# Reading a matmul's streamed columns in turns from two halves, and shifting seven weight buffers by 64 bytes

## The reference, cut to what matters

```
D_FF = 5632                                      # 44 tiles of 128
gate, up = split(h @ w_up, 2, axis=-1)           # h [256, 2048], w_up [2048, 11264]
return (gelu(dwconv_centred(gate)) * up) @ w_down    # w_down [5632, 2048]
```

## Time and profile before

| what | us |
|---|---|
| time of the kernel, median of two runs | 2174.7 (2173.54 and 2175.87) |
| span of the profiled execution | 2171.5 |
| TensorE busy with matmuls in it | 2132.8 (98%) |
| VectorE, ScalarE busy | 1464.8 (67%), 1037.6 (48%) |
| up-projection L, units 6 to 43 | about 1500 to 1920 of the span |
| down-projection M0 and M1 without the last unit | about 1920 to 2151 of the span |

### The profile page before, as it was taken

One profiled execution on the slowest core, in us unless ns is written; L12 is line 12 of the kernel. 1 busy time (PEld: TensorE's weight loads), 2 busy tenths in 40 slices (PEclk: granted clock), 3 DMA queues, 4 the chain that ended last, 5 costly groups with the idle time before them and its releaser, 6 DMA issues.

```text
span 2171.5 us, 38030 instructions
## 1 busy us (share of the span) xinstructions
PE 2132.8 (98%) x16496; PEld 1987.9 (92%) x16496; DVE 1464.8 (67%) x1850; ACT 1037.6 (48%) x1418; POOL 25.0 (1%) x47
## 2 busy tenths in 40 slices
PE   7999999999999999999999999999999999999998
PEld 7989999988999999998788999999999999988886
DVE  7666556666757698696665577789666665555665
ACT  6554334444454465454433455465444444444454
POOL 0000000110000000000000000000000000000000
PEclk9999999999999999999999999999999999999999
DMA  9765655775448878786565655766777775555553
GB/s 326 239 208 195 196 194 176 232 243 162 153 156 263 295 256 267 252 285 223 182 224 166 233 175 192 255 210 229 240 245 240 243 242 195 194 193 190 182 196 112
DMA packets 339156, 470.05 MB, mean 216 GB/s; under 512 B 14797, under 2 KB 312557, under 8 KB 326126
## 3 DMA queue, kind: packets, MB, share of 16 engines
q1 hardware_dynamic: 337838, 466.93, 64.5%
q0 software_dynamic: 1152, 0.70, 0.1%
HBM read 464.80 MB, written 2.10 MB: 215 GB/s over the span
## 4 chain that ended last, share of the span: by engine, by line
PE 91%; DVE 5%; ACT 2%; DMA 2%; issue 1%; SPq 0%; ACTq 0%; DVEq 0%
PE ps L1971 64%; PE ps L1982 11%; PE ps L1990 4%; DVE wlo L1191 2%; PE ps L2002 1%; PE ps L2060 1%; ACT whi L595 1%; DMA raw<-w_branch_dram 1%; PE ps L2321 1%; PE ps L2261 1%; PE ps L2223 1%; PE ps L2255 1%; DVE arena L1257 1%; DMA raw<-w_in_dram 1%; PE ps L1926 1%
## 5 line engine op out<-in xcount | busy, mean ns | idle before, releaser
L1191 DVE TENSOR_TENSOR wlo<-raw,whi 128x1024 fp32r<-128x1024 f32 (+1 forms) x668 | 814.6, 1221 | 661.7 <-ACT whi L595 658.5
L595 ACT ACTIVATE whi<-raw 128x1024 fp32r<-128x1024 f32 (+1 forms) x668 | 706.3, 1058 | 1065.2 <-PE ps L1971 860.5
L1971 PE MATMUL ps<-f_hi,whi 128*128 128x256 f32 x2112 | 422.0, 281 | 1.6 <-DVE f_lo L1835 1.6
L1971 PE MATMUL ps<-f_lo,whi 128*128 128x256 f32 x2112 | 413.8, 277 | 0.0
L1971 PE MATMUL ps<-f_hi,wlo 128*128 128x256 f32 x2112 | 413.5, 277 | 0.0
L1971 PEld LDWEIGHTS ps<-f_hi,whi 128*128 128x128 f32 x2112 | 320.7, 188 | 14.3 <-issue 11.8
L1971 PEld LDWEIGHTS ps<-f_hi,wlo 128*128 128x128 f32 x2112 | 319.9, 188 | 0.0
L1971 PEld LDWEIGHTS ps<-f_lo,whi 128*128 128x128 f32 x2112 | 319.9, 188 | 0.0
L1971 PE MATMUL ps<-phi,whi 128*128 128x256 f32 (+2 forms) x1440 | 300.7, 290 | 0.0
L1971 PE MATMUL ps<-plo,whi 128*128 128x256 f32 (+2 forms) x1440 | 288.4, 281 | 0.0
L1971 PE MATMUL ps<-phi,wlo 128*128 128x256 f32 (+2 forms) x1440 | 288.1, 281 | 0.0
(11 more groups left out here) (380 smaller groups left out, 2595.1 us busy)
## 6 DMA issues: line engine op xcount, KB each, us to landing
raw<-w_in_dram SPq DMA_DIRECT2D x151, 1024.0 KB, 5.9
raw<-ada_w_dram SPq DMA_DIRECT2D x96, 1024.0 KB, 5.0
raw<-ffn_w_up_dram SPq DMA_DIRECT2D x88, 1024.0 KB, 5.0
raw<-ffn_w_down_dram SPq DMA_DIRECT2D x44, 1024.0 KB, 5.2
raw<-w_out_dram SPq DMA_DIRECT2D x32, 1024.0 KB, 5.7
raw<-w_branch_dram SPq DMA_DIRECT2D x16, 1024.0 KB, 6.1
arena<-xT_dram SPq DMA_DIRECT2D x4, 544.0 KB, 6.6
arena<-ctxT_dram SPq DMA_DIRECT2D x1, 2048.0 KB, 11.1
```

Of the source, the lines that this page charges most:

```text
L595: nc.scalar.activation(whi[slot_of(c)][:, 0:w], src, ACT.Copy).then_inc(S("split_hi"), 1)
L1191: v.tensor_tensor(wlo[slot_of(c)][:, 0:w], src, whi[slot_of(c)][:, 0:w].bitcast(F32), ALU.subtract).then_inc(S("split_lo"), 1)
L1971: l = mm(ps[2 * p + h][0:m, b:b + tt.stop - tt.start], wx[:, k], x[:, xi, tt], start=first, stop=last)
```

## The change: order of the streamed columns, and buffers

1. In L, units 6 to 43, chunks q = 1 to 3, a matmul reads its 256 streamed columns no longer straight through. It reads a run from the first half of the tile, one from the second half, the next run of the first half, and so on. A run is 16 floats (64 bytes) for q = 1 and 2 and 4 floats (16 bytes) for q = 3. For q = 2 and 3 the sums are written to PSUM in the same order, so that each column lands where it did. For q = 1 the tiles `kt` 4 to 7 of `f_hi` and `f_lo` are stored in an order that makes the turned reading give the natural one, and PSUM is written straight.
2. In M0 and M1 (without the last unit) the same is done with the 512 streamed weight columns and the sums, for q = 1 to 3, with the same run lengths.
3. To store the four tiles so, ScalarE writes `f_hi` in a stepped pattern, and VectorE writes `f_lo` with two instructions of 128 columns in place of one of 256.
4. Slots 5 to 7 of `whi` and slots 4 to 7 of `wlo` start 64 bytes later, which is a multiple of 128 bytes. Slot 4 of `whi` stays. These buffers serve all phases from E on.

```diff
-        whi += [at(f"whi{4 + i}", [128, CW], MEM + RING * RW + CW * i + 16, F32R) for i in range(4)]
-        wlo += [at(f"wlo{4 + i}", [128, CW], MEM + RING * RW + CW * (4 + i) + 16, F32R) for i in range(4)]
+        whi += [at(f"whi{4 + i}", [128, CW], MEM + RING * RW + CW * i + (32 if i else 16), F32R) for i in range(4)]
+        wlo += [at(f"wlo{4 + i}", [128, CW], MEM + RING * RW + CW * (4 + i) + 32, F32R) for i in range(4)]
+
+        def turns(v, n):
+
+            return v.rearrange("p (two run n) -> p run two n", two=2, n=n)
@@ stream_hi
-                nc.scalar.activation(f_hi[:, kt, :], ptmp[:, kt % 2, 0:256], ACT.Identity, bias=shift).then_inc(S("res_hi"), 1)
+                src, dst = ptmp[:, kt % 2, 0:256], f_hi[:, kt, :]
+                if k == 1 and kt // 4 == 1:
+                    src, dst = src.rearrange("p (run two n) -> p run two n", two=2, n=16), turns(dst, 16)
+                nc.scalar.activation(dst, src, ACT.Identity, bias=shift).then_inc(S("res_hi"), 1)
@@ stream_lo
+                if k == 1 and kt // 4 == 1:
+                    src = ptmp[:, kt % 2, 0:256].rearrange("p (run two n) -> p two run n", two=2, n=16)
+                    hi, dst = f_hi[:, kt, :].rearrange("p (two run n) -> p two run n", two=2, n=16), f_lo[:, kt, :].rearrange("p (two run n) -> p two run n", two=2, n=16)
+                    v.scalar_tensor_tensor(dst[:, 0], src[:, 0], shift, hi[:, 0].bitcast(F32), ALU.add, ALU.subtract)
+                    v.scalar_tensor_tensor(dst[:, 1], src[:, 1], shift, hi[:, 1].bitcast(F32), ALU.add, ALU.subtract).then_inc(S("res_lo"), 1)
@@ chunk, the matmuls of T units
-                                l = mm(ps[2 * p + h][0:m, b:b + tt.stop - tt.start], wx[:, k], x[:, xi, tt], start=first, stop=last)
+                                moving, sums = x[:, xi, tt], ps[2 * p + h][0:m, b:b + tt.stop - tt.start]
+                                if name == "L" and not early and q:
+                                    moving = turns(moving, 4 if q == 3 else 16)
+                                    if q > 1:
+                                        sums = turns(sums, 4 if q == 3 else 16)
+                                l = mm(sums, wx[:, k], moving, start=first, stop=last)
@@ chunk, the matmuls of DN units (M0, M1)
-                                l = mm(ps[(4 if name == "M0" else 0) + 2 * t + nb][:, :], x[:, kd, 128 * t:128 * t + 128],
-                                       wx[:, 512 * nb:512 * nb + 512], start=first, stop=last)
+                                moving, sums = wx[:, 512 * nb:512 * nb + 512], ps[(4 if name == "M0" else 0) + 2 * t + nb][:, :]
+                                if q:
+                                    n = 4 if q == 3 else 16
+                                    moving, sums = turns(moving, n), turns(sums, n)
+                                l = mm(sums, x[:, kd, 128 * t:128 * t + 128], moving, start=first, stop=last)
```

More of the change, by code:

```diff
@@ L1698, in stream_lo @@
                 dve.wait_ge(S("res_hi"), 16 * k + kt + 1)
-                v.scalar_tensor_tensor(f_lo[:, kt, :], ptmp[:, kt % 2, 0:256], shift, f_hi[:, kt, :].bitcast(F32), ALU.add, ALU.subtract)\
-                    .then_inc(S("res_lo"), 1)
+                if k == 1 and kt // 4 == 1:
[3 more added lines that the diff above has]
+                    v.scalar_tensor_tensor(dst[:, 1], src[:, 1], shift, hi[:, 1].bitcast(F32), ALU.add, ALU.subtract).then_inc(S("res_lo"), 1)
+                else:
+                    v.scalar_tensor_tensor(f_lo[:, kt, :], ptmp[:, kt % 2, 0:256], shift, f_hi[:, kt, :].bitcast(F32), ALU.add, ALU.subtract)\
+                        .then_inc(S("res_lo"), 1)
                 dve.wait_ge(S("res_lo"), 16 * k + kt + 1)
```

## The result

The changed kernel takes 2224.4 us (median of two runs, 2221.39 and 2227.50) against 2174.7 us. The ratio is 1.0237, with a 95% interval of 1.0187 to 1.0287. So the change is clearly slower. The profiled execution has a span of 2225.7 us, 54.2 us more than the one before.

The account below looks back on a forecast made before the run. The prediction took TensorE's matmul pace as the bound and summed 0 + 10.1 + 1.1 + 3.5 + 1.0 = +15.7 us, taking 2174.7 to 2190 us. Its range was 2150 to 2250 us.

Parts of the forecast that it names:

- rival B: Turned reads in L, M0, M1: each change of place in memory costs time, 2220 to 2280 us; chance 0.26.
- last sign: Closing test: prediction wrong altogether if reads at a new order change the level by more than 4.5 ns.
- What bounds: Whole MLP stage: TensorE's matmul pace sets the time in both directions, in flight for 98% of the span.
- Term 1: Order of the turned reads in L, M0, M1: taken as 0, bounds -30.0 to +89.7 us.
- Term 2: Shifted buffers under turned reads in L: +3.7 ns a matmul, +10.1 us, and +1.1 us for q = 0.
- Term 3: Shifted buffers in E to OB, straight reads: low-pace chunks +5.3 us, the others -1.8 us, together +3.5 us.
- Term 4: VectorE's four split instructions storing f_lo in L: +1.0 us, bounds 0 and 1.2.
- Sum: Whole kernel: all parts together +15.7 us, from 2174.7 to 2190 us.
- Rival A: Turned reads in L, M0, M1: the time beyond one column a cycle goes, 2158 or 2150 us; chance 0.25.
- cheap end: Turned reads: leaving a 64-byte piece costs 0.41 ns in L, so only runs of 4 pay more; 2220 us.
- dear end: Turned reads: the piece is 128 bytes, 0.83 ns each, so runs of 16 pay too; 89.7 us, 2280 us.
- Rival C: Turned reads or stepped sums in L, M0, M1 run at half rate, 2333 or 2525 us; chance 0.09.

Follow-up runs that it names:

- turn_only: The changed kernel with the buffers back at their old places, so turned reads, sums' order and stepped storing alone: 2209.7 us, ratio 1.0176.
- reads_only: Kernel before with only the reads in L, M0 and M1 turned (straight, runs of 16, 4, 2 for q = 0 to 3), sums straight: 2277.7 us.
- sums_only: Kernel before with only the sums' write order turned in L, M0, M1 (straight, runs of 16, 4, 2), reads straight: 2169.6 us.
- shift_only: Kernel before with only the buffers shifted by 64 bytes (slots 5 to 7 of whi, 4 to 7 of wlo), all straight: 2203.8 us, ratio 1.0149.
- classes: Kernel before, straight reads, weight slots of q = 0 to 3 starting 0, 32, 64, 96 bytes past a multiple of 128: 2196.1 us.
- orders: Kernel before with L, M0, M1 reads and sums straight, even/odd 64-byte pieces, four quarters, even/odd 128-byte pieces for q = 0 to 3: 2200.6 us.
- pieces: Kernel before with slots 0 to 3 stored as weight pieces offset 64 bytes from their tiles, planes moved, one more wait at E: 2189.6 us, ratio 1.0076.
- before_again: The kernel before, unchanged, profiled a second time: 2174.9 us.

## Why the prediction was right or wrong

The range (2150 to 2250) holds 2224.4 and the sign was forecast, but the likeliest case said 2190, 15.7 us more than before where the medians show 49.7. The range reached that far only because it took in part of rival B, whose law turned out wrong too, so that it held is in part luck. By its last sign the prediction is wrong altogether if a new order changes the level by more than 4.5 ns, and it changed it by 6.7 and 14.3 ns. By its own steps:

1. **What bounds.** Right. All of the change is TensorE's pace in the lines named.
2. **Term 1, the order of the reads, taken as 0.** This is the step that failed. With the old buffers the table gives L 912 x 1.2 + 912 x 7.3 + 912 x 6.7 + 912 x 13.0 ns = 25.7 us and M 252 x 1.3 + 252 x 11.2 + 252 x 11.1 + 252 x 22.8 ns = 11.7 us, 37.4 us. turn_only alone is 36.8 us slower. I took the straight stream for the nearest row because the same 64-byte pieces are read once and whole. That says nothing on price: no row had a stream that leaves its order, and the value belonged between the bounds. In its place the runs show 6.7 to 7.3 ns a matmul for runs of 16 and 13.0 for runs of 4 in L, and reads_only and sums_only put them on the reads alone.
3. **Term 2, 3.7 ns for the shift in L, 11.2 us.** The mechanism was right for straight reads and a little dearer than rows 7 let expect (118.6 ns, not 117.0). Under turned reads it is nothing, and only q = 0's 3.2 ns x 912 = 2.9 us are left. I had added two costs that hide each other. The count for q = 0 was wrong as well. I charged only the 8 matmuls of a chunk whose buffer is shifted, but in shift_only all 24 run at 117.5 ns on average, 912 x 4.2 = 3.8 us and not 1.1.
4. **Term 3, E to OB, +3.5 us.** Right in sign, 9.6 us measured. The stretches at the low pace went to 118.5 ns, not 117.0, and those at 117.8 did not fall but rose (H to 45.49 / 384 = 118.5 ns, IQ to 37.00 / 312 = 118.6). The 9.6 us hold some chance too, since this stage varies by 8 us among kernels with the same code in it.
5. **Term 4, VectorE's split instructions, +1.0 us.** Nothing measured (74.0 us for 74.5).
6. **Sum.** 37.4 + 2.9 + 9.6 + 0 = 49.9 us against 15.7 forecast. With the 4.7 us ahead of E that is 54.6, and the two profiled spans differ by 54.2.

**Rival A** (0.25), the tax goes, did not happen: no order came below 113.3 ns. **Rival B** (0.26) had the right sign and near its cheap end the right size (2220). Its law was wrong. Its cheap end gave runs of 16 nothing and runs of 4 19.8 ns, its dear end 6.6 and 46.3. Measured are 6.7 and 14.3. **Rival C** (0.09) is out for reads at the lengths of the change, and for sums at every length tried (sums_only). At runs of two floats the read comes towards it: 166 ns, of the 213.3 ns that 256 columns take at two cycles each.

The Trainium skill (Advanced Engine Details and Errata, Memory Cachelines) asks for at least two hits on a 16-byte line of SBUF. By that rule runs of 16 bytes would pass at full rate. The runs show 126.3 ns for them, 120.6 for runs of 64 bytes and 113.3 for a straight stream, so the measurement decides against it here. The step to 165.3 ns for 8-byte runs, which hit a 16-byte line twice before leaving, is large. For the sums, the same page's first sentence on PSUM (any non-contiguous pattern slows matmuls significantly) is contradicted by 113.3 and 228.9 ns in sums_only. The second one, that every two consecutive elements should be contiguous, fits, but every run kept to it, so no run tests it.

The Trainium skill (TensorE: Matmul & The Clock Gate, Step-by-step: what each phase is for) says that the engine has two independent read ports for SBUF and that loading the next weights takes no read bandwidth from the running matmul. In classes nothing but the weights' start address is changed, and the stream runs at 113.3 or at about 118.5 ns. So where the weights lie does reach the stream. That it does so through the load's reads is the likely way, but it is argued and not shown: ScalarE and VectorE write to the moved addresses too.

## What to carry to other kernels

Where TensorE streams four-byte values at a column a cycle, read the moving operand straight through or in long runs. In L, runs of 64 floats from two halves cost nothing beyond the first matmuls, and shorter ones cost 5% (32), 6% (16), 9% (8), 11% (4) and 46% (2). If columns must change their order, change it on the PSUM side, where it was free down to runs of two floats. And start the weights 64 bytes past a multiple of 128 when the streamed tile starts at a multiple of 128, since the other places tried cost 4 to 5%. The good place allows the low pace and does not assure it (q = 0 of orders and the late units of pieces are in it, at 117.8 ns).

When a trace has no row for what a change does, "same bytes, other order" is not evidence for zero. Take a value inside the bounds, and ask of two costs on the same stream whether they can both be paid.

## What the runs showed of the hardware

- The straight stream's tax (113.3 ns for the 106.7 ns of 256 columns) could be raised by orders and addresses but was never lowered.
- A straight stream has two paces, 113.3 and 117.8 ns, at the same addresses (E before and in before_again, H before and in sums_only). For 512 columns they are 228.9 and 233.3 ns (M in pieces, where the planes had moved by 128 bytes). The step is 4.4 to 4.5 ns a matmul at both widths, while the tax grows with the columns (6.7 and 15.6 ns). That speaks for two origins, but no run tests it. A chunk of 24 matmuls differs by 24 x 4.5 ns = 0.11 us. The 80 chunks of E, F and OB alone can make 8.6 us, and the runs of the kernel before lay between 2167.4 and 2178.0 us. What sets the pace after a pause was not found, and so no version that forces the low one was tried.
- The pace carries over a change of order. In turn_only a straight chunk after one in runs of 4 has six matmuls at 118.4 ns on average before it is at 113.3. In orders it stays at 117.8.
- Turned reads of 16 do not react to the weights' address (120.0 with it shifted, 120.6 and 120.0 without).
- In M, where planes are the stationary operand and weights are streamed, the rule of 64 bytes does not show: classes has 229.0 ns with weights at 0 bytes and 233.1 at 64, and before has 228.9 at 64. These may be the two paces again. Which addresses count there stays open.
- No version beat the kernel before. sums_only (2169.6 us beside 2173.7) is level with it.
